# An attention pipeline that takes its heads in pairs

## What is computed

```python
q, k, v, f, g_a, g_b = project_in(modulate(y))
# latent queries: a window of the 8 x 64 grid plus all 128 context keys, 8 heads of 64
s_win = einsum('bhrqd,bhrkcd->bhrqkc', qg, k_band) + bias
s_win = where(col_ok, s_win, NEG_INF)
s_ctx = einsum('bhrqd,bhjd->bhrqj', qg, k_ctx)
p = softmax(concat([s_win, s_ctx]))
o = p_win @ v_band + p_ctx @ v_ctx
# context queries: softmax over the 128 context keys
# fourier branch: real part of an orthonormal 2-D DFT over (positions, group of 128 channels)
mix = (sigmoid(g_a) * (fourier(f) @ w_fourier) + sigmoid(g_b) * (heads(o) @ w_na_out)) @ w_out
```

## Time and profile before

| | |
|---|---|
| time, median of three runs | 2873.42 us |
| the profiled execution: time, span | 2874.3 us, 2872.4 us |
| TensorE busy | 2759.1 us, 96% |
| VectorE busy | 1681.5 us, 59% |
| ScalarE busy | 755.5 us, 26% |
| mean granted clock of TensorE | 0.985 |

### The profile page before, as it was taken

How to read it: one execution, slowest core, us unless ns; L and a number is a source line. 1 busy time by engine, 2 the same in 40 slices (tenths; PEclk the granted TensorE clock), 3 DMA queues, 4 the chain that set the end, 5 groups by cost and what they waited for, 6 DMA issues and landing times.

```text
span 2872.4 us, 47162 instructions
## 1 busy us (share of the span) xinstructions
PE 2759.1 (96%) x18676; PEld 2720.6 (95%) x18676; DVE 1681.5 (59%) x3126; ACT 755.5 (26%) x1081; POOL 0.2 (0%) x4
## 2 busy tenths in 40 slices
PE   4899999899999999999999999998999999999996
PEld 4899999899999999999999999998989999999996
DVE  6755555753756764445586555575466568535356
ACT  3211111542322431111261111134332225211113
POOL 0000000000000000000000000000000000000000
PEclk8999999999999999999999999999999999999998
DMA  6343333112233232323223333322213322323231
GB/s 251 120 125 124 120 118 117 67 48 76 84 126 113 74 107 98 109 97 111 95 68 134 121 109 119 118 81 70 71 35 134 124 95 81 110 90 125 82 128 37
DMA packets 77635, 295.12 MB, mean 103 GB/s; under 512 B 25024, under 2 KB 31424, under 8 KB 53952
## 3 DMA queue, kind: packets, MB, share of 16 engines
q1 hardware_dynamic: 51264, 210.11, 21.0%
q10 hardware_dynamic: 26240, 83.20, 8.8%
HBM read 289.61 MB, written 6.82 MB: 103 GB/s over the span
## 4 chain that ended last, share of the span: by engine, by line
PE 91%; DVE 5%; ACT 1%; issue 1%; DMA 1%; SPq 0%; ACTq 0%; DVEq 0%
PE psum L592 12%; PE psum L595 12%; PE psum L594 12%; PE psum L413 6%; PE psum L412 6%; PE psum L410 6%; PE psum L455 3%; PE psum L459 3%; PE psum L458 3%; PE psum L813 3%; PE psum L816 3%; PE psum L815 3%; PE psum L496 2%; PE psum L500 1%; PE psum L501 1%; PE psum L668 1%
## 5 line engine op out<-in xcount | busy, mean ns | idle before, releaser
L592 PE MATMUL psum<-Uh,w_hi 128*128 128x320 f32 x2304 | 712.9, 309 | 8.9 <-DVE cst_l L1480 8.9
L594 PE MATMUL psum<-Ul,w_hi 128*128 128x320 f32 x2304 | 712.7, 309 | 0.0
L595 PE MATMUL psum<-Uh,w_lo 128*128 128x320 f32 x2304 | 712.5, 309 | 0.0
L877 ACT ACTIVATE w_hi<-w_raw 128x2048 fp32r<-128x2048 f32 x166 | 317.5, 1913 | 592.6 <-PE psum L410 317.4
L592 PEld LDWEIGHTS psum<-Uh,w_hi 128*128 128x128 f32 x2304 | 433.2, 188 | 9.2 <-issue 9.2
L594 PEld LDWEIGHTS psum<-Ul,w_hi 128*128 128x128 f32 x2304 | 433.2, 188 | 0.0
L595 PEld LDWEIGHTS psum<-Uh,w_lo 128*128 128x128 f32 x2304 | 433.2, 188 | 0.0
L1205 DVE TENSOR_TENSOR w_lo<-w_raw,w_hi 128x2048 fp32r<-128x2048 f32 x166 | 380.2, 2291 | 78.5 <-ACT w_hi L877 74.2
L1392 DVE TENSOR_TENSOR hf<-sg,psum 128x320 f32<-128x320 f32 x176 | 85.6, 487 | 408.4 <-ACT sg L966 406.8
L413 PE MATMUL psum<-Hh,w_lo 128*128 128x320 f32 x1024 | 316.2, 309 | 0.0
L410 PE MATMUL psum<-Hh,w_hi 128*128 128x320 f32 x1024 | 316.2, 309 | 0.0
(11 more groups left out here) (237 smaller groups left out, 4997.1 us busy)
## 6 DMA issues: line engine op xcount, KB each, us to landing
w_raw<-in_wstream SPq DMA_DIRECT2D x184, 1024.0 KB, 4.9
ada_w<-in_ada ACTq DMA_DIRECT2D x145, 512.0 KB, 3.6
first_w<-in_ada SPq DMA_DIRECT2D x15, 512.0 KB, 14.6
gath<-in_rpb SPq DMA_DIRECT2D x128, 24.0 KB, 3.4
G<-gath ACTq DMA_DIRECT2D x4, 768.0 KB, 4.5
X<-in_xT SPq DMA_DIRECT2D x8, 320.0 KB, 14.5
yT<-X SPq DMA_DIRECT2D x16, 160.0 KB, 1.8
mask<-in_mask ACTq DMA_DIRECT2D x2, 384.0 KB, 5.0
```

What stands on the lines that cost most here:

```text
L592: m1 = pe.matmul(out, wh, rh, start=(k == 0), stop=False)
L594: pe.matmul(out, wh, rl, start=False, stop=False)
L595: mm = pe.matmul(out, wl, rh, start=False, stop=(k == KD - 1))
L877: act.activation(hi, w_raw[:, r, :, :], ACT.Copy).then_inc(s_whi, 1)
```

## The change

`UNIT` now pairs the heads: two heads of one pair for each query block, so that one step n holds units 2n and 2n + 1, one in the upper and one in the lower rows. Ten steps take the place of twenty turns. In a step TensorE issues the window scores of both units, then the context key scores of both, into PSUM banks 0 and 1, after one wait for both max of the step before; then the output products of step n - 2; then the transposes of step n - 1; then one Fourier piece, n, in each of the first eleven steps. VectorE does both max, stores piece n - 1, then takes both reciprocals, forms two bias tiles in the steps of `BIAS_STEP` (1, 2, 3, 5, 6, 7), scales the outputs of step n - 2, and has its low tiles in steps 2 and 7. ScalarE does both exps of step n, then both copies of step n - 1, and rounds a tile in steps 1 and 6. `pr`, `PT` and `bm` have four buffers, `odd` two, and the zone is laid out anew (128 bytes larger). The constants, and the three loops as they are after the change:

```diff
-PIECE_AT = {0: 0, 1: 1, 2: 2, 3: 3, 5: 4, 8: 5, 10: 6, 13: 7, 15: 8, 18: 9, 21: 10}
+BIAS_STEP = {1: 0, 2: 1, 3: 2, 5: 3, 6: 4, 7: 5}
...
-        pr = at("pr", 33280, [P, 3, 384])
-        PT = at("PT", 37888, [P, 3, 384])
...
+        pr = at("pr", 30848, [P, 4, 384])
+        PT = at("PT", 36992, [P, 4, 384])
...
+        odd = at("odd", 19456, [P, 2, HALFW])
+        bm = at("bm", 51328, [P, 4, 384])
...
-        UNIT = [(h, QB) for h in range(4)] + [(h, j) for h in range(4) for j in range(QB)]
-        N = len(UNIT)
+        UNIT = [(h, QB) for h in range(4)] + [(2 * p + e, j) for p in range(2) for j in range(QB) for e in range(2)]
+        STEPS = len(UNIT) // 2
+
+        def units(n):
+            return (2 * n, 2 * n + 1)
+
+        def bias_of(h, j):
+
+            g = 3 * (h // 2) + BIAS_KIND[j]
+            return g, 2 * (g % 2) + h % 2
...
+        for n in range(STEPS + 2):
+            if n < STEPS:
+                if n == 0:
                     pe.wait_ge(s_free, use.at(T // P))
                     pair_evacuated(0)
                 else:
+                    pe.wait_ge(s_max, C["max"].next(2))
+                if n == 2:
                     pe.wait_ge(s_att, C["att"].next(64 if hh == 0 else 32))
+                h0, j = UNIT[2 * n]
+                hp = h0 // 2
                 if j < QB:
+                    for e in range(2):
+                        po = HD * e
+                        pe.matmul(scores(e, 256), qT[po:po + HD, hp, j * P:(j + 1) * P],
+                                  kT[po:po + HD, hp, KEY0[j] * ROWS:KEY0[j] * ROWS + 256], start=True, stop=True)
+                    for e in range(2):
+                        po = HD * e
+                        pe.matmul(psum[:, e, 256:384], qT[po:po + HD, hp, j * P:(j + 1) * P],
+                                  ckT[po:po + HD, 2 * hh + hp, :], start=True, stop=True).then_inc(s_sc, 1)
                 else:
+                    for e in range(2):
+                        po = HD * e
+                        pe.matmul(scores(e, P), qT[po:po + HD, hp, LAT:T], kT[po:po + HD, hp, LAT:T],
+                                  start=True, stop=True).then_inc(s_sc, 1)
+                C["sc"].next(2)
+            if n >= 2:
+                for b in units(n - 2):
+                    h, j = UNIT[b]
+                    pe.wait_ge(s_ptc, C["ptc"].next())
+                    if b == 0:
+                        all_evacuated()
+                    if b >= 2:
+                        pe.wait_ge(s_of, C["of"].next())
+                    vt = VTILES[j] + (8,) if j < QB else (7,)
+                    for t, v in enumerate(vt):
+                        mm = pe.matmul(head_out(b), PT[:, b % 4, t * P:(t + 1) * P],
+                                       V[:, v, h * HD:(h + 1) * HD], start=(t == 0), stop=(t == len(vt) - 1))
+                    mm.then_inc(s_o, 1)
+                    C["o"].next()
+            if 1 <= n <= STEPS:
+                if n == 1:
                     pair_evacuated(1)
+                for b in units(n - 1):
+                    pe.wait_ge(s_exp, C["exp"].next())
+                    for t in range(width(b) // P):
+                        mm = pe.transpose(turned(b, t * P, (t + 1) * P), pr[:, b % 4, t * P:(t + 1) * P],
+                                          ident[:, :])
+                    mm.then_inc(s_pt, 1)
+                    C["pt"].next()
+            if n < PIECES:
+                if n < 2:
                     pair_evacuated(3)
                 else:
+                    pe.wait_ge(s_fev, C["fev"].at() + (n - 1))
+                piece(n, C["fev"].at()).then_inc(s_fill, 1)
                 C["fill"].next()
         C["max"].next(2)
         C["of"].next(2)
         C["fev"].next(PIECES)
...
+        for n in range(STEPS + 1):
+            if n < STEPS:
+                for i in units(n):
+                    w = width(i)
+                    act.wait_ge(s_max, C["max"].next())
+                    act.activation(pr[:, i % 4, 0:w], pr[:, i % 4, 0:w], ACT.Exp, bias=stat[:, i % 8, 0:1],
+                                   scale=-1.0, accum_out=stat[:, i % 8, 2:3]).then_inc(s_exp, 1)
+                    C["exp"].next()
+            if n >= 1:
+                for b in units(n - 1):
+                    w = width(b)
+                    act.wait_ge(s_pt, C["pt"].next())
+                    if b >= 4:
+                        act.wait_ge(s_o, C["o"].next())
+                    act.activation(PT[:, b % 4, 0:w], turned(b, 0, w), ACT.Copy).then_inc(s_ptc, 1)
+                    C["ptc"].next()
+            if n in (1, 6):
                 round_tile()
+        C["o"].next(4)
         use_no[0] += -use_no[0] % 4

...
+        for n in range(STEPS + 2):
+            if n < STEPS:
+                for i in units(n):
+                    h, j = UNIT[i]
+                    w = width(i)
+                    if i >= 4:
+                        dve.wait_ge(s_pt, C["pt"].next())
+                    dve.wait_ge(s_sc, C["sc"].next())
+                    b = bm[:, 0, 256:384]
+                    if j < QB:
+                        g, slot = bias_of(h, j)
+                        dve.wait_ge(s_dve, bias_at[g])
+                        b = bm[:, slot, :]
+                    mark(dve.tensor_tensor_reduce(pr[:, i % 4, 0:w], scores(i, w), b, 1.0, BIG, ALU.add, ALU.min,
+                                                  stat[:, i % 8, 0:1]), "max")
+            if 1 <= n <= PIECES:
+                store_piece(hh, n - 1)
+            if 1 <= n <= STEPS:
+                for b in units(n - 1):
+                    dve.wait_ge(s_exp, C["exp"].next())
+                    dve.reciprocal(stat[:, b % 8, 3:4], stat[:, b % 8, 2:3]).then_inc(s_dve, 1)
+                    recip_at[b] = C["dve"].next()
+            if n in BIAS_STEP:
+                if n == 1:
                     dve.wait_ge(s_att, C["att"].next(64 if hh == 0 else 32))
+                p, kind = divmod(BIAS_STEP[n], 3)
+                for h in (2 * p, 2 * p + 1):
+                    g = G[:, h, :, BIAS_OFF[kind]:BIAS_OFF[kind] + WCOLS].rearrange("p r t -> p t r")
+                    slot = 2 * (BIAS_STEP[n] % 2) + h % 2
+                    dve.tensor_tensor(bm[:, slot, 0:256].rearrange("p (t r) -> p t r", r=ROWS),
+                                      mask[:, kind, :].rearrange("p (t r) -> p t r", r=ROWS), g,
+                                      ALU.subtract).then_inc(s_dve, 1)
+                    bias_at[BIAS_STEP[n]] = C["dve"].next()
+            if n >= 2:
+                for b in units(n - 2):
+                    h, j = UNIT[b]
+                    dve.wait_ge(s_dve, recip_at[b])
+                    dve.wait_ge(s_o, C["o"].next())
+                    col = (4 * hh + h) * HD
+                    mark(dve.tensor_scalar(Otok[:, j, col:col + HD], head_out(b), stat[:, b % 8, 3:4], None,
+                                           ALU.mult), "of")
+            if n in (2, 7):
                 low_tile()
+        C["pt"].next(4)
         use_no[0] += -use_no[0] % 4

```

More of the change, by code:

```diff
@@ L125, in build @@
         epsc = sb("epsc", [P, 1])
-        zone_bytes = 92160
+        zone_bytes = 92288
         z0 = -(-nc.sbuf_base // 32) * 32
@@ L168, in build @@
         stat = at("stat", 30720, [P, 8, 4])
-        pr = at("pr", 33280, [P, 3, 384])
-        PT = at("PT", 37888, [P, 3, 384])
[L171 to L180, removed]
+        pr = at("pr", 30848, [P, 4, 384])
+        PT = at("PT", 36992, [P, 4, 384])
+        PWl = at("PWl", 43136, [P, 2, LAT], F32R)
+        CXh = at("CXh", 47232, [P, 2, 256], F32R)
+        CXl = at("CXl", 49280, [P, 2, 256], F32R)
+        odd = at("odd", 19456, [P, 2, HALFW])
+        bm = at("bm", 51328, [P, 4, 384])
+        Fh = at("Fh", 57472, [P, 5, 256], F32R)
+        Fl = at("Fl", 62592, [P, 5, 256], F32R)
+        Otok = at("Otok", 67712, [P, T // P, NA])
+        y32 = at("y32", 77952, [P, 4, T])
+        PWh = at("PWh", 88192, [P, 2, LAT], F32R)
         Oh = at("Oh", 0, [P, 4, T], F32R)
@@ L625, in attention @@
                         else:
-                            pe.wait_ge(s_max, C["max"].next())
-                        if i == 4:
+                            pe.wait_ge(s_max, C["max"].next(2))
+                        if n == 2:
                             pe.wait_ge(s_att, C["att"].next(64 if hh == 0 else 32))
+                        h0, j = UNIT[2 * n]
+                        hp = h0 // 2
                         if j < QB:
[L630 to L634, removed]
-                        else:
-                            mm = pe.matmul(scores(i, P), qT[po:po + HD, hp, LAT:T], kT[po:po + HD, hp, LAT:T],
-                                           start=True, stop=True)
@@ L638, in attention @@
[L638 to L642, removed]
-                            pair_evacuated(1)
[L644 to L649, removed]
@@ L650, in attention @@
-                    if i in PIECE_AT:
-                        f = PIECE_AT[i]
```

(23 more changed lines are left out.)

## The result

The changed kernel takes 2845.45 us, the median of four runs (2843.14 to 2847.11), against 2873.78 us for the kernel before beside it: a ratio of 0.9898, 95% interval 0.9883 to 0.9913. It is faster by some 28 us. The sign and the place were right; the gain was half as large again as the forecast.

A forecast was written before the change was run, and what follows sets the result against it. TensorE was taken to bound the kernel: its steps summed to 53.1 us a phase plus 0.9 of waits for VectorE, 54.0 against 58.5. Four phases save 17.9 us, giving 2855.5 us, range 2848 to 2867.

The forecast's parts named there:

- The sign and the place: Whole kernel: faster, chance 0.77, by 4.5 us in each of the four attention phases, 17.9 us in all.
- What bounds the phase: Attention phase: TensorE's own work end to end, busy 58.06 of 58.50 us; TensorE again the bound after the phase.
- The score block: Score matmuls of a latent pair: two row tiles overlap but start in program order, 1.05 us, 0.63 less than before.
- the bound that I had given 0.10: Rival, scores of a pair: row tiles wholly side by side, 0.84 us, phase 52.8 us, 2850.6 us in all; chance 0.10.
- Transposes: Transposes of a latent pair on TensorE: 2 x 0.30 plus 0.09 for one change to or from outputs, 0.69 us.
- Outputs: Output products of a latent pair on TensorE: 2 x 0.71 us, 1.42 us.
- The pieces: Fourier pieces on TensorE, each now followed by scores at a cost of 0.09 us: 3.07 us in steps 0 to 4.
- VectorE's tail: Behind step 7's low tile, TensorE waits for VectorE: 0.2 us before step 9, 0.6 for step 7's outputs, 0.9 in all.
- Piece 5: Step 5: its wait for piece 4's store, 2.85 us after the step began, is covered by 0.3 as TensorE arrives at 3.16.
- No overlap: Rival, scores of a pair: row tiles do not overlap, 1.48 us, phase 56.6 us, 2865.8 us in all; chance 0.22.
- VectorE as the bound: Rival, steps 2 and 7: VectorE's long steps hold TensorE, some 4.6 us a phase, no gain, 2873.8 us; chance 0.08.
- Tile changes that drain: Rival, score block: every change of row tile drains, 2.08 us a pair, phase 61.9 us, 2887 us; chance 0.07.

The follow-up runs named there:

- The first experiment: Against the changed kernel, the scores of a latent pair are issued one head after the other: score block 0.85 us, second phase 51.32 us.
- the run with the old pieces: Against the changed kernel, the Fourier pieces are given out to the steps as before the change: second phase 55.19 us against 51.29.

## Why the prediction was right and wrong

**What bounds the phase** was right: TensorE end to end, and the gain was kept after the phase.

**The score block** was the step that failed, with the transposes and outputs mis-sized behind it. I took 1.05 us from "matmuls start in the order of the program" and measured 0.85, the bound that I had given 0.10. The order in which the trace of before showed starts was no evidence, as in it no two matmuls that follow each other use different rows. The first experiment shows that the order does not bind across row tiles. The same mistake made me charge 0.62 us for a context pair and argue from the spacing of weight loads: it measured 0.42. Term by term that is 8 x 0.20 + 2 x 0.20 = 2.0 us a phase.

**Transposes** were mis-sized: 0.69 forecast, 0.58 measured, 1.1 us a phase with those of the context pairs (0.20 and 0.15 for 0.30 each). I counted a change of form that costs nothing, and charged each unit 0.30 us, which contained some 0.05 for standing behind scores that the pair's place behind the outputs avoids.

**Outputs** came to 1.35 to 1.39 us and, at the end, 1.28 for 1.42: 0.5 us. My 0.71 a unit contained the 0.1 that scores behind them cost. **The pieces** took 0.2 us less in all (token pieces 3.03 to 3.05 for 3.07). That a piece followed by scores costs 0.1 us was right: the last pass of a wave piece starts at 618.98, the spacing is 0.23, and the scores start at 619.31.

**VectorE's tail** was right in mechanism and place for step 9 and missed step 8. I forecast 0.2 us before step 9, 0.6 for its outputs, 0.9 in all; the trace has 0.4 and 0.8 there and 0.3 ahead of step 8's outputs, 1.5 in all and 1.7 from start to start. That it is more because the shorter score blocks bring TensorE to each wait sooner fits the run with both heads in the same rows, where 0.1 is left.

**Piece 5** I had covered by 0.3 us. TensorE reaches it 0.3 us sooner than forecast (2.82 us after the step's start for 3.16), and piece 4's store is done later (3.04 for 2.85): the transposes of step 5 take 0.80 us to that piece instead of 0.58, a wait of 0.2 that I had put at nothing.

Counted from start to start in the second phase, these terms close the account. The forecast's steps add up to 53.2 (I wrote 53.1), with the tail 54.1 us; less 2.0 for scores, 1.1 for transposes, 0.5 for outputs and 0.2 for pieces, and more 0.8 for the tail and 0.2 for piece 5, that is 51.3, as measured.

**The first phase** is 1.0 us longer than the second. I took ScalarE as no bound because of its total work and did not follow the first exp: its table load stands behind two DMA issues, and when the second of them is slow (1.42 us here), one step of TensorE is now shorter than that chain.

**The rivals.** No overlap was 56.6 us a phase and the run that made it so had 55.2, by the same errors in the other terms. VectorE as the bound did not come, but the run with the old pieces shows how near it is. Tile changes that drain are excluded: a block of two tiles takes no longer than a block of one (0.85 against 0.84 us).

## What to carry to other kernels

When two matmuls fill half the rows each, issue them next to one another, here into different banks: in this kernel they cost as much as one, and the two orders tried made no difference. Then look at the engine that follows, since it sees its work come in bursts: spread the filler work evenly over the steps, and take long instructions out of the steps in which the bound engine is short. Look for small waits in the starts too, since a table of waits can miss them (0.6 us a phase here). Price a form of instruction where it stands, by the start of the next one, and do not carry an entry cost from one neighbour to another.

## What the runs showed of the hardware

- Float matmuls in the upper and the lower 64 rows run side by side from the first pass on: a pair of heads takes 0.85 us, one head 0.84, both in the same rows 1.50.
- Their starts are not bound by the program's order across the two halves of the rows: with the context matmul of the first head standing ahead, the second head's window passes still came before it, and the block was 0.85 us.
- A run of 64 row matmuls costs about 0.2 us inside its block (0.11 at the first pass and 0.09 after the last), in line with the earlier trace rows. Some 0.1 us stands ahead of the block (618.98 plus 0.23 to 619.31), and the next form's first pass is some 0.05 us longer. Between outputs and transposes, both of full height, nothing shows.
- The issue of one and the same DMA on ScalarE's queue took 0.62 us in some profiles and 1.42 to 1.91 us in others (`new_v`, ahead of the first phase), and the load of the function table starts only behind it.
